# Banded attention pairs in batches of two blocks, with the next pair's query projection interleaved and the half swap done by transfer

## The reference

```python
# layer loop of second_block, branch C
h = rmsnorm_2(x, norm_g[layer])
u = jnp.einsum('bsd,dc->bsc', h, w_in[layer])      # (..., qc, kc, vc, zc, ...)
qc_h = apply_rope(qc.reshape(b, seq, C_Q_HEADS, HEAD_DIM), cos, sin)
kc_h = apply_rope(kc.reshape(b, seq, C_KV_HEADS, HEAD_DIM), cos, sin)
yc, _ = banded_attention(qc_h, kc_h, vc_h, SWA_WINDOW - 1, sinks[layer]...)
yc = yc.reshape(b, seq, C_W) * jax.nn.silu(zc)
...
# apply_rope, per head of 64: x1, x2 are its two halves of 32
return jnp.concatenate([x1 * c - x2 * s, x2 * c + x1 * s], axis=-1)
...
# banded_attention, per block of 128 queries against 256 keys (the block before and its own)
s = jnp.where(valid, einsum(qb, kb) * scale, -inf)
m = jnp.maximum(jnp.max(s, axis=-1, keepdims=True), sink)
p = jnp.exp(s - m)
denom = jnp.sum(p, axis=-1, keepdims=True) + jnp.exp(sink - m)
out = einsum(p / denom, vb)
```

## Time and profile before

| what | us |
|---|---|
| median of 3 runs | 3416.67 |
| lowest and highest run | 3413.94, 3421.68 |
| span of the profiled execution | 3412.5 |
| PE busy in it | 3254.9 (95%) |
| DVE, POOL, ACT busy | 1971.0, 1622.7, 1055.3 |
| branch C of layer 0 (2104.28 to 2246.76) | 142.48 |
| branch C of layer 1 (3068.93 to 3211.45) | 142.52 |

### The profile page before, as it was taken

The page is one execution under the profiler, slowest core; times in us unless marked ns, Lnnn a source line. Parts: engine busy times, 40 slices in busy tenths (PEclk is TensorE's granted clock), DMA queues, the critical chain, the costliest instruction groups (busy, mean ns, idle before and its releaser), DMA issues.

```text
span 3412.5 us, 55095 instructions
## 1 busy us (share of the span) xinstructions
PE 3254.9 (95%) x22070; PEld 2604.8 (76%) x22070; DVE 1971.0 (58%) x2678; ACT 1055.3 (31%) x1725; POOL 1622.7 (48%) x903
## 2 busy tenths in 40 slices
PE   7999789898999999999999999999999999999997
PEld 6878688687888888787877777678878877776786
DVE  7445644648877777883344554566752256444665
ACT  4212344223323333344332232320343233322301
POOL 3333334146777676657822222257478422222475
PEclk9999899999999999999999999999999999999998
DMA  3121100221111111112331211143223311111332
GB/s 137 44 91 44 56 4 4 85 83 53 53 55 41 54 55 55 50 62 99 143 107 44 56 52 47 38 163 121 99 105 106 119 45 50 43 44 50 136 124 87
DMA packets 88252, 247.68 MB, mean 73 GB/s; under 512 B 13072, under 2 KB 24048, under 8 KB 86144
## 3 DMA queue, kind: packets, MB, share of 16 engines
q1 hardware_dynamic: 69664, 189.34, 16.5%
q10 hardware_dynamic: 18400, 55.63, 5.0%
HBM read 191.28 MB, written 42.12 MB: 68 GB/s over the span
## 4 chain that ended last, share of the span: by engine, by line
PE 85%; DVE 8%; ACT 2%; issue 2%; POOL 2%; DMA 0%; DVEq 0%; POOLq 0%; SPq 0%; ACTq 0%
PE ps L943 30%; PE ps L1480 11%; PE ps L1650 9%; PE ps L1510 6%; PE ps L1934 5%; PE ps L1955 4%; PE ps L1740 3%; PE ps L1767 3%; PE ps L1785 3%; DVE sc L3811 2%; PE ps L1255 1%; PE ps L1533 1%; PE ps L1231 1%; PE ps L1618 1%; POOL unit_lo L834 1%
## 5 line engine op out<-in xcount | busy, mean ns | idle before, releaser
L688 POOL TENSOR_TENSOR wH<-wraw,pv 128x1024 fp32r<-128x1024 f32 x135 | 267.0, 1978 | 1221.5 <-PE ps L943 1097.7
L943 PE MATMUL ps<-hH,wH 128*128 128x512 f32 x1488 | 473.9, 400 | 26.3 <-DVE hL L3041 11.7
L943 PE MATMUL ps<-hL,wH 128*128 128x512 f32 x1488 | 466.6, 395 | 0.0
L943 PE MATMUL ps<-hH,wL 128*128 128x512 f32 x1488 | 465.2, 394 | 0.0
L3368 DVE TENSOR_TENSOR xT<-ps,xT 128x512 f32<-128x512 f32 x544 | 366.1, 690 | 60.9 <-PE ps L1510 54.8
L690 POOL TENSOR_TENSOR wL<-wraw,wH 128x1024 fp32r<-128x1024 f32 x135 | 353.7, 2620 | 10.6
L943 PEld LDWEIGHTS ps<-hH,wH 128*128 128x128 f32 x1488 | 274.5, 189 | 88.8 <-issue 17.9
L943 PEld LDWEIGHTS ps<-hL,wH 128*128 128x128 f32 x1488 | 277.8, 189 | 59.0 <-issue 1.7
L943 PEld LDWEIGHTS ps<-hH,wL 128*128 128x128 f32 x1488 | 277.7, 189 | 57.5 <-issue 0.3
L2689 ACT ACTIVATE sc<-sc,stat 128x256 f32<-128x256 f32 (+7 forms) x256 | 171.1, 669 | 163.1 <-DVE stat L3818 102.1
L1767 PE MATMUL ps<-cst,sc 128*128 128x128 f32 x900 | 148.7, 285 | 12.5 <-ACT pt L2709 8.4
(11 more groups left out here) (545 smaller groups left out, 7244.0 us busy)
## 6 DMA issues: line engine op xcount, KB each, us to landing
wraw<-ws SPq DMA_DIRECT2D x158, 512.0 KB, 3.5
gates<-gated SPq DMA_DIRECT2D x48, 512.0 KB, 2.7
sg<-gates SPq DMA_DIRECT2D x16, 1536.0 KB, 6.5
upA<-ws SPq DMA_DIRECT2D x42, 256.0 KB, 3.3
upB<-ws SPq DMA_DIRECT2D x42, 256.0 KB, 2.6
gateA<-ws SPq DMA_DIRECT2D x40, 256.0 KB, 3.5
gateB<-ws SPq DMA_DIRECT2D x40, 256.0 KB, 2.7
xT<-park ACTq DMA_DIRECT2D x2, 4096.0 KB, 12.1
```

What stands on the lines that cost most here:

```text
L688: pool.tensor_tensor(wH[:, j, :], wraw[:, j, :], zero, ALU.add).then_inc(w_hi, 1)
L943: mm = pe.matmul(pair(p)[:, half * HALF:(half + 1) * HALF], wp, hp[:, k, half * HALF:(half + 1) * HALF], start=(m == 0 and n == 0), stop=( ...
```

## The change

Branch C gets functions of its own on PE, ACT and DVE (`band_pair`, `band_query`); `head_pair` is left for A and B. It does four things.

1. **Batches of two.** The scores of blocks 2b and 2b+1 are written together, side by side in banks 0 and 1. PE waits for all four maxima of the batch before. DVE starts on a block of even number only when the odd one's scores of the same head are written too. Transposes and values go in twos as well.
2. **Half slots.** A z or a query slot is made as 24 products for tokens 0 to 511 into one bank and then 24 for the others into the next (`half_slot`): z in banks 2 and 3, and then the queries of the next pair in the same banks. The first pair's queries go to banks 4 and 5.
3. **Next pair's queries beside this pair.** The query products of pair i+1 are spread between this pair's later blocks, so only the third pair is without them.
4. **Half swap by transfer.** PE's `rotate` is gone. For each half of the tokens ACT copies the queries (128x512) and starts four transfers of 32 partitions each into `qswap`; DVE makes the rope of that half from it.

```diff
@@ score_bank @@
-    return j * (HALF if br == "C" or n < 4 else 2 * HALF)
+    if br == "C":
+        return j * HALF + n % 2 * 2 * P
+    return j * (HALF if n < 4 else 2 * HALF)
...
@@ PE @@
-            def rotate(p, src):
...
+            def half_slot(j, use, banks, half_done):
+
+                def products(h, m0, m1):
...
+                    for m in range(m0, m1):
+                        k, n = divmod(m, 3)
+                        w, x = ((wH, hH), (wH, hL), (wL, hH))[n]
+                        mm = pe.matmul(bank(banks[h]), w[:, j, k * P:(k + 1) * P], x[:, k, halves(h)],
+                                       start=(m == 0), stop=(m == 3 * KT - 1))
...
             def window_keys(L):
...
-                pe.wait_ge(sem("a_raw"), L * 14 + 11)
+
+                pe.wait_ge(sem("rec_copied"), spreads(L, BAND_FIRST))
+                q = half_slot(0, band_use(L, 0), (4, 5), "qc_half")
+                q(0, 0, 8)
                 pe.wait_ge(sem("at_y"), pi + 1)
                 pe.wait_ge(sem("a_v"), L * 6 + 6)
                 value_transposes(3)
+                q(0, 8, 24)
+                q(1, 0, 24)
...
+                def scores(b):
+
+                    if b == 2:
+                        pe.wait_ge(sem("a_rope"), band_rope(L, i, 1) + 1)
+                    if b:
+                        pe.wait_ge(sem("at_max"), last + 4 * b + 2)
...
+                def first_transposes():
+                    pe.wait_ge(sem("rec_copied"), spreads(L, i + BAND_FIRST))
+                    pe.wait_ge(sem("a_vtok"), L * 6 + 6)
+                    transposes(0)
...
+                bank_free(0)
+                if i == 2:
+                    z(0, 0, 3)
+                    first_scores()
+                    z(0, 3, 18)
+                    scores(1)
+                    first_transposes()
+                    z(0, 18, 24)
...
+                z(0, 0, 4)
+                first_scores()
+                z(0, 4, 20)
+                scores(1)
+                first_transposes()
+                z(0, 20, 24)
+                bank_free(1)
+                z(1, 0, 14)
+                scores(2)
+                first_values()
+                transposes(1)
+                z(1, 14, 24)
+                pe.wait_ge(sem("zc_in"), since("zc_in", L * 3 + i + 1))
+                q(0, 0, 8)
+                scores(3)
+                values(1)
+                transposes(2)
+                q(0, 8, 24)
+                pe.wait_ge(sem("a_z"), pi * 2 + 1)
+                q(1, 0, 6)
+                transposes(3)
+                q(1, 6, 20)
+                values(2)
+                values(3)
+                pe.wait_ge(sem("at_rec"), pi + 1)
+                pe.transpose(bank(4)[0:16, 0:P], stat[:, S_REC, :], ident).then_inc(sem("at_rows"), 1)
+                q(1, 20, 24)
...
@@ ACT @@
+            def band_query(L, i, h):
+
+                if i:
+                    act.wait_ge(sem("a_rope"), band_rope(L, i - 1, h) + 1)
+                if h == 0:
+                    act.wait_ge(sem("qc_half"), since("qc_half", L * 3 + i + 1))
+                else:
+                    act.wait_ge(gemm_done[0], band_use(L, i) + 1)
+                act.activation(qraw3[:, halves(h)], bank(2 + h if i else 4 + h), ACT.Copy, scale=0.125).then_inc(sem("a_raw"), 1)
+                act.wait_ge(sem("a_raw"), band_raw(L, i, h))
+                act.wait_ge(sem("a_rot"), band_swaps(L, i, h))
+                for a in range(4):
+                    b = a ^ 1
+                    act.dma_start(qswap[32 * a:32 * a + 32, halves(h)], qraw3[32 * b:32 * b + 32, halves(h)]
+                                  ).then_inc(sem("a_rot"), 16)
...
+                exponentials(7)
+                sinks()
...
+                band_query(L, i + 1, 0)
+                copy_transposed(6)
+                band_query(L, i + 1, 1)
+                spread_reciprocals(L, i + BAND_FIRST)
...
@@ DVE, band_pair @@
+                        dve.wait_ge(sem("at_S"), pi * 16 + s + (1 if n % 2 else 3))
...
+                maxima(0)
+                maxima(1)
+                band_query(L, i, 1)
+                maxima(2)
+                maxima(3)
+                copy_transposed(1)
+                gate_input(0)
...
+                output_gate()
+                reciprocals()
+                copy_transposed(7)
+                band_query(L, i + 1, 0)
+                output()
```

More of the change, by code:

```diff
@@ L1697, in gate_phase @@
                         pe.sem_inc(gemm_done[1], 1)
-            def rotate(p, src):
-                for half in range(2):
-                    mm = pe.matmul(pair(p)[:, half * HALF:(half + 1) * HALF], cst[:, C_ROT, :],
-                                   src[:, half * HALF:(half + 1) * HALF], start=True, stop=True)
-                mm.then_inc(sem("a_rot"), 1)
             def value_transposes(p):
@@ L1795, in period @@
                         return
[L1796 removed]
+                    if n < 7 and n != 3:
                         scores(n + 1)
@@ L1906, in head_pair, with first_scores @@
-                ends_here = br == "C" and i == 2
-                for n in range(within, 8 if ends_here else 7):
+                    if leading:
+                        wait(pe, "g_in", L, PLAIN + 2 * GATE_PAIRS)
+                    value_transposes(2)
+                def first_scores():
+                    if br == "B":
+                        pe.wait_ge(sem("a_rope"), L * 13 + i * 2 + 2)
+                    pe.wait_ge(sem("a_raw"), raw + 2)
+                    scores(0)
+                within = 3
@@ L1908, in head_pair @@
+                for n in range(within, 7):
                     period(n)
-                if ends_here:
-                    rows()
-                    values(7)
             def branches(L, d):
@@ L2028, in layer_loop @@
                         window_keys(L)
+                        for i in range(count):
+                            band_pair(L, i)
+                        continue
                     if br != "B":
@@ L2751, in unmask @@
+                if br == "A" and i == 0:
+                    first_values(L)
+                if br == "A" and i:
+                    output_hi(L, i + (first - 1))
+                if br == "B" or i:
+                    act.wait_ge(gemm_done[slots[2][0]], slots[2][1] + 1)
+                    if br == "B":
+                        act.wait_ge(sem("a_rope"), L * 13 + i * 2 + 1)
+                    act.activation(vst2[:, :], pair(0), ACT.Copy).then_inc(sem("a_v"), 1)
                 def unmask(n):
```

500 lines of the change are left out of this document (308 added, 192 removed).

## The result

The changed kernel takes 3379.82 us (median, 3376.25 to 3386.50), the kernel before 3416.52 beside it. The sign was right, and so were the rotation and the idle time that it named. Half of the gain came from something that it had priced at nothing, and behind the stage came a small wait that it had priced at nothing too.

What follows compares the result with a forecast made beforehand. PE was taken as the bound, busy 3254.9 of 3412.5 us. A layer: -5.2 rotation, -6.6 idle time, +2.9 head waits, +0.3 small waits, -8.6; two layers -17.2, from 3416.7 to 3399.5, own range 3394 to 3404.

Steps and rivals of the forecast that it cites:

- the rotation: PE's rotation products in branch C go: three pairs by 1.72 us, 5.2 us a layer less.
- what neither gains nor costs: Part on branch C's products: half slots keep their pitch, and scores, transposes and values are as many; no change in time.
- the second sum: Check of branch C's length from piece durations times their number: 134.1 against 142.5 us, or -8.4 a layer.
- Old idle time: PE's waits in branch C's stage: 5.4 us a layer shown plus 1.2 estimated as hidden; nearly all 6.6 goes.
- the heads' waits: PE waits for ACT's exponentials at the start of pairs 1 and 2: 1.2 and 1.7, together 2.9 us a layer added.
- The walk: Step-by-step timing of a pair's head: ACT is free at 6.3 to 6.4 us after the first z product, then exponentials follow.
- The half slot's pitch: 24 products in a row into one bank take 0.2276 us each, as before; no cost.
- The first pair's first scores: The one narrow place: queries' rope ready at 1.1 us against 0.9 wanted; no wait taken, 2.1 a layer if POOL's lock hits.
- No cost, 5 us of room: Behind the stage, gate loads start later but land at +6 us, and PE wants them at +10.9.
- better: Rival, 0.07: ACT issues its transfers faster or PE's head waits overlap; -11 us a layer, 3394.7.
- ordering slips: Rival, 0.17: pair 0 pays the DVE/POOL lock, 2.1 us, and reciprocals' stores land later; -5.5 a layer, 3405.7.
- The slower one: Rival, 0.06: ACT's issuing at pair heads delays everything; gain gone at 4.3 us more a head, 3424 with 6 more.

Runs made afterwards that it cites:

- e6_single_trips: The changed kernel with single blocks in all batches, each block's scores waiting for the maxima of the block before; 3400.12 us, ratio 0.9953 to the kernel before.

## Why the prediction was wrong in size

The step that failed is the sentence "Scores, transposes and values are as many as before", under what neither gains nor costs, and with it the second sum, which multiplied 0.63, 0.37 and 0.59 by the number of blocks (15.2 a pair). The pieces are as many, but a duration in the earlier trace rows holds 0.15 to 0.20 for a change of the array's division, and the batches have fewer of them. Counted in the code's order, a pair before has 32 changes: two around the first scores, two in the first block's period, four in each of six periods, and four around the last two blocks' values. After it has 12: 2, 2, 3, 3 and 2. In time that is 5.3 against 2.1 a pair, so 9.6 a layer and 19 in all (the third pair, which has its rows among the values, differs a little); the traces have 8.4 and 10.1 less busy time beyond the rotation, 9.9 and 10.1 without the lower clock. The count fits other kernels too: from the changed kernel to `e6_single_trips` it is 30 changes a layer more, 12 by 0.20 and 18 by 0.15, or 5.1, and PE's busy time in layer 1 is 5.1 more. The term was sized at 0. The second sum even added "about 1.0 where pieces of different kinds meet" to durations that held the price already.

The trace of before held it: four projection products at 0.93 behind transposes and 1.12 behind values, two transposes at 0.37 or 0.22. The sums from two sides agreed because they shared the error.

The other terms, a layer, in layer 0 and layer 1:

- Rotation, forecast 5.2: right, by putting it back (5.7 in the chain, of which 0.6 is the change of division).
- Old idle time less the heads' waits, forecast 6.6 - 2.9 = 3.7: 3.4 and 4.4 by the idle times. The size is right, though the 6.6 holds 1.2 that is drawn as busy. The heads alone, forecast 2.9, were 4.4 and 2.0 by taking them out, with the 1.5 of the clock in the 4.4, which the prediction hadn't foreseen. The walk had both pairs' exponentials at 6.3 to 6.4; the third pair's came at 7.3 in layer 0, since the store landed 2.4 and not 1.4 after its issue.
- The half slot's pitch, no cost: right.
- The first pair's first scores, no cost: right, but narrowly. The second rope step starts 0.75 ahead of z's first product, where the walk had the swap's landing 0.4 ahead, and the last one comes 0.17 before POOL's request:

```profile
2133.51 0.69 DVE L3913 TENSOR_TENSOR qP<-qP,qswap 128x512 f32<-128x512 f32 x1
2133.68 2.27 POOL L725 TENSOR_TENSOR wH<-wraw,pv 128x1024 fp32r<-128x1024 f32 x1 [7.11 <-PE ps L1750]
```

So it was POOL that waited: 2.27 against 1.89 undisturbed. In layer 1 DVE was ahead by 0.28. The scores stand right behind the projection products. The fixed part of about 2 us that the Trainium skill states for a transfer ("SBUF — State Buffer", section "The DMA setup-cost knee") agrees with the swap's 2.0. The store of 8 KB landed in 1.4, which is below it, and there the measurement decides.
- "No cost, 5 us of room" behind the stage: wrong by 1.9 in layer 0 and 0.5 in layer 1. The room was counted for the gates' data, but a weight slot stood behind them in SP's queue.

Of the rivals, "better" had the right side with 0.07, but not the cause: four transfers issue in 2.44 against 2.50. Of "ordering slips", the lock was missed by 0.17 us, and the store landed late in one of four heads. The slower one did not come: a head cost 1.0 to 1.5 us in waits, not 4.3 more than forecast.

The measured terms are -5.2 for the rotation, -3.9 of idle time and -9.3 for the changes less the clock (means of the two layers), -18.4 a layer. They are cut from the same stage lengths, so that they add up is no proof. Both layers make -36.7, and with +2.4 behind the stage -34, against 33.6 in the spans and 36.7 in the medians.

## What to carry to other kernels

Price small products not by their number but by the order they stand in: read the same kind of product behind different neighbours, and take the difference as the price of the change. Where PE also waits for a round trip, half of such a saving was paid out as a wait here; group the blocks so that both fall together. A second sum from the same rows is no second opinion.

## What the runs showed of the hardware

- A change between whole array, half its rows and half its columns costs PE 0.15 us into transposes or values and 0.20 to 0.22 into scores or projection products; a change of kind, or a return to the same bank, within one division costs nothing (0.11 for a transpose by turns with whole products, 0.26 by turns with half-row ones).
- Half-row products that take the two row halves and two banks by turns have twice the rate of those that stay in one half and one bank: 0.108 against 0.216 an instruction, at 256 columns. Which of the two matters was not tried apart.
- Eight changes of division in 4 us, with PE busy throughout, were followed by a granted clock of 0.50 in layer 0's first pair; the same products in two runs, in runs of 2, or as whole-array products by turns left it at 1.00 in that stage.
- Behind a wait of 1.5 us at a pair's head the granted clock was 0.59 over 3.8 us, and cost 1.5 us; waits of 0.5 at the same place of layer 1 left it at 1.00.
- VectorE and GpSimd hold each other up in operations with two SBUF operands, whichever comes second: GpSimd's split took 2.27 instead of 1.89 when VectorE's step had begun 0.17 before it, and VectorE's step took 2.02 when the split had begun first, against 1.22 for one of its size.
- A swap of 64 KB lands in 2.0, of 128 KB in 2.3.
